# Block inverse on packed 64x64 diagonal blocks, multiplied on quarters of TensorE's array

## The reference

```python
C = DN_CHUNK                     # 64
L = jnp.where(strict, jnp.einsum('bhnid,bhnjd->bhnij', k_beta, k) * decay, 0.0)
rhs = jnp.concatenate([v * beta[..., None], k_beta * jnp.exp(g)[..., None]], axis=-1)
sol = lax.linalg.triangular_solve(L + jnp.eye(C, dtype=L.dtype), rhs, left_side=True,
                                  lower=True, unit_diagonal=True)
u, w = sol[..., :dv], sol[..., dv:]
...
def step(state, xs):             # chunk after chunk
    v_new = u_c - einsum(w_c, state)
    o = einsum(qd_c, state) + einsum(a_c, v_new)
    state = state * exp(gl_c) + einsum(kd_c, v_new)
```

## Time and profile before

| | |
|---|---|
| median of 3 runs | 966.14 us (965.4 to 966.41) |
| the profiled execution | 966.55 us, of which the span of the profile is 964.5 us |
| PE busy | 946.8 us (98% of the span), 5717 matmul records |
| DVE, ACT, POOL busy | 672.0, 514.4, 30.7 us |
| granted PE clock | 0.998 of full speed over the span |

### The profile page before, as it was taken

The page is one execution under the profiler, slowest core; times in us unless marked ns, Lnnn a source line. Parts: engine busy times, 40 slices in busy tenths (PEclk is TensorE's granted clock), DMA queues, the critical chain, the costliest instruction groups (busy, mean ns, idle before and its releaser), DMA issues.

```text
span 964.5 us, 14527 instructions
## 1 busy us (share of the span) xinstructions
PE 946.8 (98%) x5717; PEld 839.9 (87%) x5717; DVE 672.0 (70%) x855; ACT 514.4 (53%) x696; POOL 30.7 (3%) x48
## 2 busy tenths in 40 slices
PE   8999999999999999999999999999999999999997
PEld 8999998888888887899988888888898788888885
DVE  5766776789888887776668756657768476565664
ACT  5765564666656657444446444444656564444443
POOL 2100000200000000000000000001010000000000
PEclk9999999999999999999999999999999999999999
DMA  9933223566565654645546566566444446565631
GB/s 290 274 113 107 88 66 99 175 190 215 184 207 176 216 167 143 214 152 190 180 138 203 200 192 200 174 194 198 113 128 165 131 164 207 187 203 181 210 133 44
DMA packets 118398, 164.31 MB, mean 170 GB/s; under 512 B 14510, under 2 KB 96875, under 8 KB 118219
## 3 DMA queue, kind: packets, MB, share of 16 engines
q1 hardware_dynamic: 116731, 158.52, 50.8%
q0 software_dynamic: 1312, 4.74, 1.6%
q10 hardware_dynamic: 304, 0.33, 0.1%
HBM read 162.53 MB, written 1.05 MB: 170 GB/s over the span
## 4 chain that ended last, share of the span: by engine, by line
PE 93%; DVE 2%; DMA 2%; ACT 1%; issue 1%; POOL 0%; POOLq 0%; DVEq 0%; ACTq 0%
PE ps L281 19%; PE ps L992 19%; PE ps L283 18%; PE ps L282 18%; PE ps L989 9%; PE ps L2075 3%; PE ps L1449 2%; DMA raw<-in_w_in_dram 1%; PE ps L2070 1%; PE ps L1470 1%; PE ps L1333 1%; PE ps L543 1%; PE ps L1459 0%; DMA X<-in_x_dram 0%; DVE hT L502 0%
## 5 line engine op out<-in xcount | busy, mean ns | idle before, releaser
L237 DVE TENSOR_TENSOR w_lo<-raw,w_hi 128x2048 fp32r<-128x2048 f32 (+1 forms) x146 | 330.5, 2265 | 120.8 <-ACT w_hi L223 120.7
L223 ACT ACTIVATE w_hi<-raw 128x2048 fp32r<-128x2048 f32 x147 | 278.7, 1896 | 105.2 <-PE ps L283 100.3
L992 PE MATMUL ps<-hT,w_hi 128*128 128x512 f32 x768 | 241.2, 395 | 0.0
L989 PEld LDWEIGHTS ps<-hT,w_lo 128*128 128x128 f32 x768 | 144.0, 188 | 33.5
L281 PE MATMUL ps<-w_hi,act_hi 128*128 128x512 f32 x416 | 162.8, 391 | 0.0
L283 PE MATMUL ps<-w_lo,act_hi 128*128 128x512 f32 x416 | 162.0, 389 | 0.0
L282 PE MATMUL ps<-w_hi,act_lo 128*128 128x512 f32 x416 | 161.9, 389 | 0.0
L989 PE MATMUL ps<-hT,w_lo 128*128 128x256 f32 x768 | 151.1, 278 | 0.0
L281 PE MATMUL ps<-hT,w_hi 128*128 128x256 f32 x424 | 122.2, 288 | 1.4 <-DVE hT L502 0.9
L282 PE MATMUL ps<-hT,w_lo 128*128 128x256 f32 x424 | 119.9, 283 | 0.0
L283 PE MATMUL ps<-hT,w_hi 128*128 128x256 f32 x424 | 119.8, 283 | 0.0
(11 more groups left out here) (322 smaller groups left out, 1062.0 us busy)
## 6 DMA issues: line engine op xcount, KB each, us to landing
raw<-in_mlp_w_dram SPq DMA_DIRECT2D x64, 1024.0 KB, 5.4
raw<-in_w_up_dram SPq DMA_DIRECT2D x22, 1024.0 KB, 5.1
raw<-in_a_w_in_dram SPq DMA_DIRECT2D x16, 1024.0 KB, 5.5
raw<-in_w_in_dram SPq DMA_DIRECT2D x11, 1024.0 KB, 6.5
raw<-in_w_down_dram SPq DMA_DIRECT2D x11, 1024.0 KB, 5.0
raw<-in_a_w_out_dram SPq DMA_DIRECT2D x8, 1024.0 KB, 4.9
raw<-in_w_out_dram SPq DMA_DIRECT2D x4, 1024.0 KB, 5.0
raw<-in_b_w_o_dram SPq DMA_DIRECT2D x4, 1024.0 KB, 4.9
```

The source lines that it names most:

```text
L223: nc.scalar.activation(w_hi[:, s, 0:n], raw[:, r, 0:n], ACT.Copy).then_inc(hi_ready, 1)
L237: nc.vector.tensor_tensor(w_lo[:, s, 0:n], raw[:, r, 0:n], w_hi[:, s, 0:n].bitcast(F32), ALU.subtract).then_inc(lo_ready, 1)
L989: nc.tensor.matmul(banks[:, b + t, S:2 * S], w_l[:, k, t * P:(t + 1) * P], hT[:, k, 0, :], start=k == 0, stop=False, skip_group_check=True)
L992: mm = nc.tensor.matmul(banks[:, b + t, :], w_h[:, k, t * P:(t + 1) * P], hT[:, k, :, :].rearrange("p x s -> p (x s)"), start=False, stop= ...
```

## The change

Since the chunks have 64 positions, the inverse is block diagonal with 64x64 blocks up to level 5. The changed kernel keeps only these blocks:

- `Ec` and `Dc` replace `Em` and `Dm` in levels 1 to 5. `Ec` is 128 x 8 x 64: its partitions 0 to 63 hold the first chunk's block of each matrix, 64 to 127 the second's. `Dc` is 128 x 4 x 128 (a matrix of blocks beside each other). Both lie in the space of the old `Dm`.
- `turn_compact` does 4 transposes of 128x128, each of two matrices' blocks, in place of 8.
- The 8 products of 128x128x128 become 16 of 64x64x64, each on a quarter of the array: rows (operand partitions) 0 to 63 or 64 to 127, columns (output partitions) 0 to 63 or 64 to 127. They take the quarters in turn, in the order of `TILES`.
- `lower_copies` is one copy of 128x512 in place of two; `masked` and `upper` are two operations of 128x256 in place of two of 128x512.
- In level 0, L2549's two operations of 128x512 become four of 64x256.
- Level 6 forms only its one off-diagonal block: 8 quarter matmuls in front and 8 in back, a plain copy in place of the mask, and two negations of 64x256 into `Em`. ACT's `whole_copies` puts the diagonal blocks into `Em` (two copies of 64x512), DVE clears `Em`'s lower left quarter once at the stage's start.
- Semaphore counts follow: `level_back` waits for both masked parts at once, and both of a front's signals are set by its last matmuls.

Everything between the steps keeps its place in each stream.

```diff
-LEVELS = 7
+LEVELS = 6
...
         def level_mask(lv):
-            return msk[:, 3 + lv, :].unsqueeze(1).to_broadcast([P, NH, P])
+            if lv == 0:
+                return msk[:, 3, :].unsqueeze(1).to_broadcast([P, NH, P])
+            return msk[:, 3 + lv, 0:CH].unsqueeze(1).to_broadcast([P, NH, CH])
+
+        dm = Dm.rearrange("p g e -> p (g e)")
+        Dc = dm[:, 0:512].rearrange("p (t e) -> p t e", t=NH)
+        Ec = dm[:, 512:1024].rearrange("p (g e) -> p g e", g=G8)
+        Yc = Ym[:, 0:4, :].rearrange("p g e -> p (g e)").rearrange("p (c t e) -> p c t e", c=2, t=NH)
+        HALF = (slice(0, CH), slice(CH, P))
+        TILES = [(t, c, j) for t in range(NH) for c, j in ((0, 0), (1, 1), (0, 1), (1, 0))]
...
+            def turn_compact(lv):
+                pe.wait_ge(v_u, 2 * lv)
+                for t in range(NH):
+                    tr = pe.transpose(DT[0][:, t * P:(t + 1) * P], Ec[:, 2 * t:2 * t + 2, :].rearrange("p g e -> p (g e)"), ident[:])
+                tr.then_inc(v_d, 1)
+
             def level_front(lv):
-                for tb in range(TB):
-                    pe.wait_ge(v_u, 2 * (lv - 1) + tb + 1)
-                    turn(DT[tb], Em, tb, v_d)
-                for tb in range(TB):
-                    products(YE[tb], Lm, Em, tb, v_y)
+                turn_compact(lv)
+                for t, c, j in TILES:
+                    mm = nc.tensor.matmul(YE[c][HALF[j], t * CH:(t + 1) * CH], Lm[HALF[c], 2 * t + j, HALF[c]], Ec[HALF[c], 2 * t + j, :],
+                                          start=True, stop=True)
+                    if t == NH - 1 and (c, j) in ((0, 1), (1, 0)):
+                        mm.then_inc(v_y, 1)
 
             def level_back(lv):
-                for tb in range(TB):
-                    pe.wait_ge(v_m, 2 * (lv - 1) + tb + 1)
-                    pe.wait_ge(v_dc, 2 * (lv - 1) + tb + 1)
-                    products(YE[tb], Dm, Ym, tb, v_e)
+                pe.wait_ge(v_m, 2 * lv)
+                pe.wait_ge(v_dc, lv)
+                for t, j, c in TILES:
+                    mm = nc.tensor.matmul(YE[j][HALF[c], t * CH:(t + 1) * CH], Dc[HALF[j], t, HALF[c]], Yc[HALF[j], c, t, :],
+                                          start=True, stop=True)
+                    if t == NH - 1 and (c, j) in ((0, 1), (1, 0)):
+                        mm.then_inc(v_e, 1)
+
+            def last_front():
+                turn_compact(LAST)
+                for t in range(NH):
+                    for j in range(2):
+                        mm = nc.tensor.matmul(YE[1][HALF[j], t * CH:(t + 1) * CH], Lm[HALF[1], 2 * t + j, HALF[0]],
+                                              Ec[HALF[1], 2 * t + j, :], start=True, stop=True)
+                mm.then_inc(v_y, 1)
+
+            def last_back():
+                pe.wait_ge(v_m, 2 * LAST - 1)
+                pe.wait_ge(v_dc, LAST)
+                for t in range(NH):
+                    for j in range(2):
+                        mm = nc.tensor.matmul(YE[j][HALF[0], t * CH:(t + 1) * CH], Dc[HALF[j], t, HALF[0]], Yc[HALF[j], 0, t, :],
+                                              start=True, stop=True)
+                        if t == NH - 1:
+                            mm.then_inc(v_e, 1)
...
-            for tb in range(TB):
-                pe.wait_ge(v_u, 2 * LAST + 1 + tb)
+            pe.wait_ge(v_u, 2 * LAST + 2)
+            pe.wait_ge(v_dc, LAST + 1)
+            for tb in range(TB):
...
             def lower_copies(lv):
-                for tb in range(TB):
-                    act.wait_ge(v_d, 2 * lv + tb + 1)
-                    nc.scalar.copy(Dm[:, gs_(tb), :], four(DT[tb])).then_inc(v_dc, 1)
+                act.wait_ge(v_d, lv + 1)
+                nc.scalar.copy(Dc, four(DT[0])).then_inc(v_dc, 1)
+
+            def whole_copies():
+                for c in range(2):
+                    last = nc.scalar.copy(Em[HALF[c], :, HALF[c]], Ec[HALF[c], :, :])
+                last.then_inc(v_dc, 1)
...
             def masked(lv):
-                for tb in range(TB):
-                    dve.wait_ge(v_y, 2 * lv + tb + 1)
-                    nc.vector.tensor_tensor(Ym[:, gs_(tb), :], four(YE[tb]), level_mask(lv), ALU.mult).then_inc(v_m, 1)
+                for c in range(2):
+                    dve.wait_ge(v_y, 2 * lv + c + 1)
+                    nc.vector.tensor_tensor(Yc[:, c, :, :], quarter(YE[c]), level_mask(lv), ALU.mult).then_inc(v_m, 1)
 
             def upper(lv):
-                for tb in range(TB):
-                    dve.wait_ge(v_e, 2 * (lv - 1) + tb + 1)
-                    nc.vector.tensor_tensor(Em[:, gs_(tb), :], Em[:, gs_(tb), :], four(YE[tb]), ALU.subtract).then_inc(v_u, 1)
+                for j in range(2):
+                    e = Ec.rearrange("p (t j) e -> p t j e", j=2)[:, :, j, :]
+                    dve.wait_ge(v_e, 2 * (lv - 1) + j + 1)
+                    nc.vector.tensor_tensor(e, e, quarter(YE[j]), ALU.subtract).then_inc(v_u, 1)
+
+            def last_masked():
+                dve.wait_ge(v_y, 2 * LAST + 1)
+                nc.vector.tensor_copy(Yc[:, 0, :, :], quarter(YE[1])).then_inc(v_m, 1)
+
+            def last_upper():
+                for j in range(2):
+                    dve.wait_ge(v_e, 2 * (LAST - 1) + j + 1)
+                    nc.vector.tensor_scalar(Em[HALF[0], j::2, HALF[1]], quarter(YE[j])[HALF[0]], -1.0, None, ALU.mult).then_inc(v_u, 1)
```

More of the change, by code:

```diff
@@ L1984, in level_mask, with quarter @@
         def level_mask(lv):
-            return msk[:, 3 + lv, :].unsqueeze(1).to_broadcast([P, NH, P])
+            if lv == 0:
[7 more added lines that the diff above has]
+        TILES = [(t, c, j) for t in range(NH) for c, j in ((0, 0), (1, 1), (0, 1), (1, 0))]
+        def quarter(bank):
+            return bank[:, 0:NH * CH].rearrange("p (t e) -> p t e", t=NH)
         def mix_groups():
@@ L2010, in mix_groups @@
             return out
-        LAST = LEVELS - 1
+        LAST = LEVELS
         QB, K0, K1, ZB, KB, VB, KAVA, QA, Q0, Q1, V0, V1, Z1, O0 = range(14)
@@ L2196, in query_keys @@
             def query_keys(tb):
-                pe.wait_ge(v_dc, 2 * LAST - 1 + tb)
+                pe.wait_ge(v_dc, LAST)
                 for h, g, hs in heads(tb):
@@ L2206, in query_sums @@
                 return mm
-            level_front(LAST)
+            last_front()
             for tb in range(TB):
                 query_keys(tb)
-            level_back(LAST)
+            last_back()
             pe.wait_ge(d_si, 5)
@@ L2436, in mix_act @@
             lower_copies(LAST - 1)
+            whole_copies()
             act.wait_ge(e_p, 7)
@@ L2461, in mix_dve @@
             u0 = first_unit["mix"]
+            nc.vector.memset(Em[HALF[1], :, HALF[0]], 0.0)
             nc.vector.memset(kaZ, 0.0)
@@ L2545, in mix_dve @@
             split_lo(dve, u0 + KAVA + 3)
-            idb = ident[:].unsqueeze(1).to_broadcast([P, NH, P])
             for tb in range(TB):
                 dve.wait_ge(v_y, tb + 1)
-                nc.vector.tensor_tensor(Em[:, gs_(tb), :], idb, four(YE[tb]), ALU.subtract).then_inc(v_u, 1)
+                for c in range(2):
+                    idb = ident[HALF[c], HALF[c]].unsqueeze(1).to_broadcast([CH, NH, CH])
+                    unit_less = nc.vector.tensor_tensor(Ec[HALF[c], gs_(tb), :], idb, four(YE[tb])[HALF[c], :, HALF[c]], ALU.subtract)
+                unit_less.then_inc(v_u, 1)
             split_lo(dve, u0 + QA + 3)
@@ L2599, in mix_dve @@
             values(1)
-            masked(LAST)
+            last_masked()
             keys()
-            upper(LAST)
+            last_upper()
             queries(0)
@@ L2836, in constants @@
         below = (r % 2 == 1) & (c == r - 1)
-        t[:, T_LEV + lv * P:T_LEV + (lv + 1) * P] = below.T if lv else below
+        within = below[0:CH, 0:CH].T
+        t[:, T_LEV + lv * P:T_LEV + (lv + 1) * P] = np.tile(within, (2, 2)) if lv else below
     q, k = i[:, None], np.arange(S)[None, :] - P
```

## The result

| | before | after |
|---|---|---|
| median | 965.77 us (4 runs, 965.12 to 966.41) | 956.99 us (4 runs, 956.23 to 958.53) |
| the profiled execution | 966.55 us | 956.23 us (span 954.3) |

The ratio is 0.9915, with a 95% interval of 0.9903 to 0.9926 (the two medians divided give 0.9909), so the change makes the kernel 8.8 us faster. The forecast was 959.3 us with a range of 957.8 to 964.2: the sign and most of the mechanism were right, but the median came out 0.8 us under the range.

The account below looks back on a forecast made before the run. PE was taken to be the bound with little to spare. Of 11.4 us of PE work saved, 4.6 become waits; seven items sum to -6.8 us, from 966.14 to 959.3 us, range 957.8 to 964.2.

Parts of the forecast that it names:

- groups of 2.1 us: Rival for the quarter groups: passes average 0.054 us like L1470's, so no measurable change (965.6 us); chance 0.09.
- PE slower than before: Rival: on a row half passes do not run beside other loads or passes; group 3.86 us, total +19 (985); chance 0.11.
- Item 5: Front 4 and back 4: all of PE's saving counts, -1.90 us, since DVE is busy for 7.21 of 11.40 us.
- item 6: Back 4 to group 3's turning: ACT loses one copy (-0.5), a later upper(4) eats 0.1; -0.40 us.
- the first two: Estimates for a group of 32 passes: 0.83 us with four quarters beside each other, 1.3 us with less overlap.
- the same list: The seven items from front 1 to level 6, summed to -6.8 us; at groups of 0.83 us, -8.0 (958.1).
- items 2, 4 and 6: Back 1 to group 1's turning, -0.30 us; scores to group 2's turning, -0.45; back 4 to group 3's turning, -0.40.
- the second column: Result table's column giving the forecast's seven items with the group at 0.83 us; sum -8.0 us.
- the 0.37 of entry and exit: Price in us taken for entering and leaving each quarter group, from L1470's row, where groups came to 0.39 and 0.35.
- item 3: Back 2: PE's saving counts in full, -0.73 us.
- level 6: Item 7, front 6 and back 6: -1.87 us, with 0.03 left for query_keys waiting on ACT's copy.
- the likeliest case: The forecast itself, quarter groups of 0.83 to 1.3 us, total 958.1 to 960.8 us; chance 0.65.

Follow-up runs that it names:

- the same moves: Kernel before with three pieces of ACT or DVE work moved later and a PE projection half moved ahead of group 2's turning: 965.29 us, ratio 0.9997.
- group 1's split: Changed kernel with ACT's weight-unit split moved behind group 1's scale and DVE's reciprocal ahead of its convolution taps: 954.82 us.
- level 3's split: Changed kernel with DVE's weight-unit split moved behind level 3's mask and group 2's reciprocal: 955.68 us.
- mask twice: Changed kernel with DVE's two masks of levels 1 to 5 done twice, once into unused space: 957.41 us.
- the square: Changed kernel with ACT's square of the queries moved from ahead of group 3's scale to behind the copy of level 6: 957.35 us.
- copy twice: Changed kernel with ACT copying the transposed blocks twice in each of six levels, once into unused space: 959.05 us.
- two by two: Changed kernel with the quarter changed after every second matmul in levels 1 to 5, instead of every matmul: 958.59 us.
- products twice: Changed kernel with every group of quarter matmuls of levels 1 to 5 issued twice over: 957.96 us.
- all four moves: Changed kernel with both splits and the square moved later, and a PE projection half put ahead of group 2's turning: 952.53 us, ratio 0.9865 to before.

## Why the prediction was right and where it was wrong

**Right: what bounds the kernel.** PE was the bound with little to spare. With the same moves, before gained nothing and after 4.5 us.

**Right: how a quarter works.** A step of 0.058 us (forecast 0.056), several starts within 0.02 us, DVE's operations at 0.42. Level 6's 16 passes on two quarters last as long as 32 on four, as forecast (PE's timeline of after):

```profile
124.36 0.68 PE L2179 MATMUL ps<-union 64*64 64x64 f32 x16
```

The rivals fell: groups of 2.1 us (measured 0.83), and PE slower than before, which needed passes that do not overlap at all.

The floor of about 25 ns between the starts of two matmuls, which the Trainium skill states in TensorE: Matmul & The Clock Gate, in the section on 56 ns, did not hold between quarters: by an estimate from that page 32 passes would last 0.80 us, and the whole group stands within 0.63. Here the measurement decides.

**Right: the loops.** The waits came where they were expected: 1.88 us before L1459 of group 1 (forecast 1.6), 1.69 at back 3 and group 2 (1.5), 1.59 around back 5 and group 3 (1.5), released by ACT and DVE as said. The edits to group 1's split and level 3's split showed the first two, mask twice the inside of the second; the square showed the third by its stretch.

**Right in its number, not in its path: the third loop.** Item 5 says of front 4 and back 4 "Their fills have room", and looked at DVE alone. ACT's chain to group 3's turning starts ahead of back 4, so that back 4 could not count on its own, a case that the prediction names itself ("a loop that I took as loose (back 4 or 5) closes too"). That the two items still add up to -2.90 us, for -2.75 at the measured group, is luck. In the chain one copy went (0.5 us), as item 6 says, but so did a wait of ACT for DVE of 0.51 us ahead of group 3's exponentials and about 0.2 us of slack at the turning; the last 0.1 of its 1.36 us stays open.

**Wrong: the size of the group, 1.05 us.** The step that failed is "I take 1.05 us, midway between the first two". Measured is 0.83, the lower end, at which the same list gives -8.0, 958.1 us: still inside the range. The reason given there, that nothing in the row suggests that row halves would differ, spoke for the end and not for the middle. It carries 1.2 of the 2.3 us between forecast and median.

**Wrong: the slack at the turnings**, another 0.4 us (items 2, 4 and 6 against the second column: -0.30, -0.20, +0.10). "The 0.17 us between is what a wake-up costs: no slack at all" took a gap in a row in which PE never waited for the price of a wake-up. Timelines of ACT and PE in after show it where PE does wait:

```profile
83.73 1.71 ACT L2363 ACTIVATE act_tmp<-act_tmp,a_mx 128x256 f32<-128x256 f32 x4 [0.24 <-DVE a_mx L2357]
...
100.28 1.28 ACT L2363 ACTIVATE act_tmp<-act_tmp,a_mx 128x128 f32<-128x128 f32 x4 [0.92 <-DVE a_mx L2355]
```

The scales end at 85.44 and 101.56, and PE starts at 85.49 and 101.61: 0.05 us. So there were 0.42 us of slack ahead of group 1 and 0.12 ahead of group 2. For group 2 a mask pair of 0.75 us instead of 1.28 does the rest: 0.12 + 0.53 = 0.65, the measured term. DVE's timeline of after, for 103.97 in the earlier trace rows:

```profile
99.22 0.75 DVE L2538 TENSOR_TENSOR union<-ps,union 128x256 f32<-128x256 f32 x2
```

For group 1, 0.18 is left of 0.60; 0.09 of it is that ACT waits 0.24 us for the reciprocal instead of 0.33, and the other 0.09 stay open.

**Wrong: the neighbours**, 0.4 us. I charged the 0.37 of entry and exit to each group. Back 2 and front 4 lie next to `at_out`, which pays that price itself on the side they share. PE's timeline of after, the place of the earlier trace rows:

```profile
89.38 1.15 PE L1470 MATMUL ps<-act_f,union 128*64 128x128 f32 x16
90.45 0.69 PE L2170 MATMUL ps<-union 64*64 64x64 f32 x32
91.08 0.39 PE L281 MATMUL ps<-hT,w_hi 128*128 128x256 f32 x1
```

L1470 takes 1.07 us to the next row, as it did ahead of a whole matmul (1.08), and the group saves 1.17 us of 1.80 there and not 0.95; of item 3's and item 5's surplus over the second column, 0.16 + 0.25, this is the likely cause. It is read from the rows, not tested by an edit.

**Terms that roughly held**: group 3 gave -0.30 for -0.40, level 6 -2.04 for -2.15 at the measured group. What remains is 0.37 us, by which the median of before itself lay lower in four runs (965.77) than in the three that the forecast started from.

Why the range missed: its lower end, 957.8, was the likeliest case's best sum, 958.1, less 0.3 us for a lower entry price, as though the slacks had no error of their own. With 0.2 us more at each of three loops and at the neighbours it would have reached 957.0.

## What to carry to other kernels

When a packed form is twice as fast on the engine that bounds, look where that engine takes over from the others, and list the slack there before adding up the work: here 5.4 of 14.1 us became waits. Then move what stands ahead of those waits; such moves are worth nothing before the change and 4.5 us after, so try them with it and not alone. When passes go to parts of the array, let consecutive matmuls name different parts: the same 16 matmuls took 0.63, 0.69 or 1.47 us by their order alone.

## What the hardware showed that I had not expected

**Four starts within 0.02 us.** A single instruction stream fed four quarters at 32 passes in 0.63 us, one in 0.02 us on average.

**PE's clock fell after a wait, in some executions.** In six profiles, of six different kernels, PE waited 1.77 to 1.89 us ahead of group 1's turning. In three of them (copy twice, square later, two by two) the granted clock then fell to the lower level, 1.2 GHz, for some 3 us; in three (after, level 3's split later, mask twice) it stayed at 1.00. With a wait of 0.95 us (products twice), 0.2 or none it did not fall in any. Windows of copy twice, whose wait ended at 85.74, columns as in the earlier trace rows:

```profile
86.00:87.00 1.00, 1.00 (x9) 1.00 (x7) 0.78 (x3) 1.00 (x3) 0.00 (x0) 0.62 0.00 0
87.00:88.00 1.00, 1.00 (x7) 1.00 (x6) 0.00 (x0) 0.70 (x2) 0.00 (x0) 0.50 0.81 90
...
89.00:90.00 1.00, 1.00 (x7) 1.00 (x7) 0.00 (x0) 0.00 (x0) 0.00 (x0) 0.68 0.97 401
```

and of after, where the wait ended at 85.49:

```profile
86.00:87.00 1.00, 1.00 (x11) 1.00 (x10) 0.54 (x2) 0.77 (x2) 0.00 (x0) 1.00 0.14 12
```

The last number but two of a row is the clock. In copy twice the projections' passes stood 0.21 us apart in that spell instead of 0.12, and from group 1's turning to group 2's it took 17.67 us, with the extra copies, where after took 16.12; in the square's run, which has nothing changed in that stretch, 17.71. So such a spell costs about 1.6 us. It may be what made one run of after 958.53 us long, with a mean clock of 0.996 against 0.998 in the other three. But that run left no rows to show it, and a mean clock of 0.997 stands over products twice too, whose rows have no such spell. What decides between the two outcomes is open, and no one kernel's rows show both; all four moves, which takes the wait away, has runs only 0.2 us apart.
